# Moving the low-half subtraction of the first block's input-projection weights from VectorE to GpSimd

## What is computed

```python
def hybrid_mixer(x, w_in, sc_conv_w, attn_sink, cc_conv_w, cc_conv_b, cc_ln_g, cc_ln_b, w_out):
    z = x @ w_in                                   # 1024 x 2048
    sc_b, sc_c, sc_h, q, k, v, cc_a, cc_gate = jnp.split(z, IN_OFFSETS, axis=-1)
    y_sc = sc_b * depthwise_conv(sc_c * sc_h, sc_conv_w)          # 3 taps
    q, k = rope(q), rope(k)
    y_att = banded_window_attention(q, k, v, attn_sink)           # 8 heads, window 128
    u = cc_a * jax.nn.sigmoid(cc_gate)
    u = depthwise_conv(u, cc_conv_w) + cc_conv_b                  # 31 taps
    y_cc = jax.nn.silu(layer_norm(u, cc_ln_g, cc_ln_b))
    return jnp.concatenate([y_sc, y_att, y_cc], axis=-1) @ w_out
```

## Time and profile before

| | |
|---|---|
| median of three runs | 3438.07 us |
| the profiled execution, first to last instruction | 3433.0 us |
| rest of the device time, as median less span | 5.1 us |
| TensorE busy | 3345.7 us (97%) |
| VectorE busy | 1783.2 us (52%) |
| ScalarE busy | 1340.6 us (39%) |
| GpSimd busy | 62.8 us (2%) |
| first mixer, from its norm to the next MLP | about 370 to 560 us |
| second mixer | about 1317 to 1505 us |

### The profile page before, as it was taken

The page is one execution under the profiler, slowest core; times in us unless marked ns, Lnnn a source line. Parts: engine busy times, 40 slices in busy tenths (PEclk is TensorE's granted clock), DMA queues, the critical chain, the costliest instruction groups (busy, mean ns, idle before and its releaser), DMA issues.

```text
span 3433.0 us, 38143 instructions
## 1 busy us (share of the span) xinstructions
PE 3345.7 (97%) x15584; PEld 2742.5 (80%) x15584; DVE 1783.2 (52%) x2728; ACT 1340.6 (39%) x2144; POOL 62.8 (2%) x65
## 2 busy tenths in 40 slices
PE   9999989999999999899999999999999989999999
PEld 7888767888888887678888788777888778778887
DVE  4333785533363337855433775647444765655443
ACT  3222555322242225553322554434322565434332
POOL 0000100000000001000000000000000000000000
PEclk9999999999999999999999999999999999999999
DMA  5332311333333333123333333222333313223332
GB/s 159 98 98 88 85 50 56 105 98 98 93 90 100 94 91 87 47 59 105 108 95 92 92 92 105 86 59 80 104 95 96 86 56 98 69 62 105 98 98 68
DMA packets 604286, 304.10 MB, mean 89 GB/s; under 512 B 43600, under 2 KB 601808, under 8 KB 603984
## 3 DMA queue, kind: packets, MB, share of 16 engines
q1 hardware_dynamic: 604112, 301.66, 30.7%
HBM read 299.52 MB, written 2.10 MB: 88 GB/s over the span
## 4 chain that ended last, share of the span: by engine, by line
PE 82%; DVE 10%; ACT 6%; issue 1%; DMA 0%; SPq 0%; DVEq 0%; ACTq 0%
PE ps L1762 26%; PE ps L1763 25%; PE ps L1770 25%; DVE Y L2345 1%; DVE wl L2170 1%; DVE tmp L2179 1%; ACT wh L1944 1%; PE ps L1778 1%; PE ps L1929 1%; PE ps L1913 1%; ACT tmp L2021 1%; PE ps L1831 1%; ACT tmp L2014 1%; DVE HLa L2174 0%; ACT HHa L1950 0%
## 5 line engine op out<-in xcount | busy, mean ns | idle before, releaser
L1770 PE MATMUL ps<-XL,wh 128*128 128x512 f32 (+1 forms) x2856 | 1059.5, 381 | 0.5 <-DVE XL L2246 0.5
L1762 PE MATMUL ps<-XH,wh 128*128 128x512 f32 (+1 forms) x2624 | 1044.2, 399 | 15.3 <-DVE wl L2170 6.6
L1763 PE MATMUL ps<-XH,wl 128*128 128x512 f32 (+1 forms) x2624 | 1016.8, 388 | 0.0
L2170 DVE TENSOR_TENSOR wl<-raw,wh 128x1024 fp32r<-128x1024 f32 (+1 forms) x565 | 681.8, 1210 | 536.0 <-ACT wh L1944 535.4
L1944 ACT ACTIVATE wh<-raw 128x1024 fp32r<-128x1024 f32 (+1 forms) x565 | 585.3, 1039 | 566.6 <-PE ps L1770 537.0
L1770 PEld LDWEIGHTS ps<-XL,wh 128*128 128x128 f32 x2856 | 537.1, 188 | 104.7 <-DVE XL L2246 1.1
L1762 PEld LDWEIGHTS ps<-XH,wh 128*128 128x128 f32 x2624 | 494.2, 188 | 132.7 <-issue 14.7
L1763 PEld LDWEIGHTS ps<-XH,wl 128*128 128x128 f32 x2624 | 494.3, 188 | 99.5 <-issue 3.3
L1762 PE MATMUL ps<-HHa,wh 128*128 128x512 f32 x1088 | 428.2, 394 | 5.8 <-DVE HLa L2174 5.8
L1763 PE MATMUL ps<-HHa,wl 128*128 128x512 f32 x1088 | 423.7, 389 | 0.0
L1770 PE MATMUL ps<-HLa,wh 128*128 128x512 f32 x1088 | 407.9, 389 | 0.0
(11 more groups left out here) (333 smaller groups left out, 3066.5 us busy)
## 6 DMA issues: line engine op xcount, KB each, us to landing
raw<-in_ffn_w_gu SPq DMA_DIRECT2D x176, 512.0 KB, 3.8
raw<-in_w_ff SPq DMA_DIRECT2D x128, 512.0 KB, 4.1
raw<-in_ffn_w_down SPq DMA_DIRECT2D x64, 512.0 KB, 3.9
raw<-in_w_xkv SPq DMA_DIRECT2D x32, 512.0 KB, 3.9
raw<-in_ev_w_in SPq DMA_DIRECT2D x25, 512.0 KB, 3.9
raw<-in_ffn_w_down SPq DMA_DIRECT2D x32, 384.0 KB, 3.4
raw<-in_w_in SPq DMA_DIRECT2D x24, 512.0 KB, 3.9
raw<-in_w_out SPq DMA_DIRECT2D x64, 128.0 KB, 2.7
```

What stands on the lines that cost most here:

```text
L1762: e.matmul(bank[:, c], t.wh[u % SPL][:, k, :], h[:, c], start=first, stop=False, skip_group_check=True)
L1763: e.matmul(bank[:, c], t.wl[u % SPL][:, k, :], h[:, c], start=False, stop=False, skip_group_check=True)
L1770: m = e.matmul(bank[:, 0:n], t.wh[u % SPL][:, k, :], l, start=False, stop=last, skip_group_check=True)
L2170: self.e.tensor_tensor(wl, raw, f32(wh), ALU.subtract).then_inc(self.s["lo"], self.tag("lo", f"lo.{i}"))
```

## The change

For units of `w_in` the low-half subtraction is emitted by `Pool.split_unit` and no longer by `Vector.split_unit`. It signals on a semaphore of its own, `lop`. All other weights keep their subtraction on VectorE. `p_zero` on GpSimd waits in addition for all earlier subtractions of GpSimd. With 16 units in each of two layers, 32 of the 565 subtractions move.

```diff
+LOW_ON_POOL = ("w_in",)
-SEMS = ["mm", "pe", "hi", "act", "lo", "dve", "pool", ...]
+SEMS = ["mm", "pe", "hi", "act", "lo", "lop", "dve", "pool", ...]
@@ class Pool
+    def split_unit(self, i):
+        nk, r, s = self.units_in[i][3], i % RAW, i % SPL
+        if self.units_in[i][0] not in LOW_ON_POOL:
+            return
+        wh, wl, raw = (x[:, 0:nk, :] for x in (self.t.wh[s], self.t.wl[s], self.t.raw[r]))
+        self.hold.wait_ge(*self.at(f"hi.{i}"))
+        self.e.tensor_tensor(wl, raw, f32(wh), ALU.subtract).then_inc(self.s["lop"], self.tag("lop", f"lo.{i}"))
@@ Pool.p_zero
         self.hold.wait_ge(*self.own("pool"))
+        self.hold.wait_ge(*self.own("lop"))
         self.e.memset(ap, 0.0).then_inc(self.s["pool"], self.tag("pool", k))
@@ class Vector, split_unit
+        if self.units_in[i][0] in LOW_ON_POOL:
+            return
```

More of the change, by code:

```diff
@@ L193, in vec @@
         return self.VT[:, V_OFF[name] + i:V_OFF[name] + i + 1]
-SEMS = ["mm", "pe", "hi", "act", "lo", "dve", "pool", "ct", "mem", "out", "rga", "rgb", "pos"]
+SEMS = ["mm", "pe", "hi", "act", "lo", "lop", "dve", "pool", "ct", "mem", "out", "rga", "rgb", "pos"]
 SEMS += [f"raw{i}" for i in range(RAW)] + [f"x{k}" for k in range(KD)]
```

## The result

| | median | runs | ratio to before | 95% interval |
|---|---|---|---|---|
| before | 3437.33 us | 4 | | |
| changed | 3452.89 us | 4 | 1.0043 | 1.0031 to 1.0056 |

The changed kernel is 15.6 us slower; 3453 had been forecast. Its profiled execution has a span of 3449.9 us, 16.9 more than before. One execution, of 17298 us in the run with quarters for the 6th to 13th unit, is left out of its ratio.

The account below looks back on a forecast made before the run. TensorE was taken to bound the whole span, but in the mixers the chain through VectorE and ScalarE. Per mixer 1.5 + 0.2 + 3 + 2.9 = 7.6 us, 15 us for both, gave 3453 us, range 3430 to 3478.

Parts of the forecast that it names:

- The mutual exclusion: In the mixers, a GpSimd subtraction holds up VectorE's two-SBUF-input work for its 2.5 us, less one-input work or idle time.
- PSUM-reading instructions named as free: Masked maximum L2321, L2189, L2224 and L2306 read one operand from PSUM and should pass beside GpSimd's subtraction.
- one-input work: VectorE instructions with one input were to run unhindered under GpSimd's subtraction, shortening the 2.5 us hold-up.
- The price of a subtraction: One 128x1024 subtraction on GpSimd was put at 2.3 to 2.6 us, taken as 2.5, twice VectorE's 1.23.
- mean over 2.5 us: Sign of being right: GpSimd's group of subtractions has a mean over 2.5 us.
- The end of the MLP: GpSimd's last sum for the mean queues behind the third unit's subtraction, delaying VectorE's closing sum: +1.5 us a mixer.
- the worst rival: Full stalls: taps always pay the full time, or TensorE, idling more, loses clock; 3470 us, chance 0.13.
- Start of the projection: The fourth subtraction would end at about 393.6, TensorE wants it at 393.5: +0.2 us a mixer.
- 401 to 428 us: Subtractions from the sixth unit on stall rotations, the first score and centring, less VectorE's savings: +3 us a mixer.
- 428 to 519 us: Six units, eleventh to sixteenth, stalls less savings, the eleventh worst (+1.3), the thirteenth best (-0.25): +2.9 us a mixer.
- 9.0 us of relief: Eight of a mixer's sixteen subtractions stand on the chain at 1.13 us each; moving them frees at most 9.0 us.
- 14.9 us of stalls: VectorE standing still beside GpSimd's subtractions from 401 us on, per mixer: 14.9 us, 5.9 net of relief.

Follow-up runs that it names:

- the run with quarters for the 6th to 13th unit: Changed kernel, but only the 6th to 13th w_in unit of a layer subtracted on GpSimd, in four pieces of 256 columns; others on VectorE: 3435.8 us.
- the run without reads: Changed kernel, but for w_in units GpSimd writes zeros into the low-half tile (four half clears) instead of subtracting: 3427.6 us, ratio 0.9973.
- eighths: Changed kernel, but first three w_in units on VectorE and 4th to 16th on GpSimd in eight pieces of 128 columns: 3435.5 us, ratio 0.9991.

## Why the prediction was right

**The mutual exclusion** was the step on which the sign hung, and it held: 3427.6 us without the reads, 3452.9 with them. The PSUM-reading instructions named as free passed; the masked maximum (17 of them from 400 to 530 us in `tmp<-ps,CT`) kept 483 ns. That they should pass was the author's estimate, with no row beside it. The trace of the kernel before has such a case, GpSimd with four copies and VectorE with a subtraction that reads PSUM:

```profile
2897.89 2.30 POOL L2157 COPY M<-XM 128x512 f32<-128x512 f32 x4 [218.27 <-PE ps L1831]
```

```profile
2898.38 0.69 DVE L2174 TENSOR_TENSOR HLa<-ps,HHa 64x512 fp32r<-64x512 f32 x1 [9.79 <-ACT HHa L1950]
```

It took 0.69 us, the median of the 48 of this kind. What the prediction had wrong is that one-input work passes too: two such instructions took 2.09 us for 0.49 and 2.26 us for 0.23, as shown below. The prediction and the expectations speak of a port; the runs show that the two engines exclude each other (2.78 us for 0.69), and not by what.

**The price of a subtraction** was taken as 2.5 us. The fastest took 2.36, the median was 2.40, and the mean of 2.48 contains GpSimd's own waits for VectorE: eight of the 32 took 2.55 to 2.85 us. The mean over 2.5 us that was named as a sign of being right did not come, the other signs did.

**The end of the MLP** is the mis-sized term: 1.5 us forecast, 2.3 and 3.4 measured. The wait was right: the last sum ends late and the closing sum waits for it.

```profile
370.28 1.26 POOL L2156 TENSOR_TENSOR tmp<-tmp,XR 128x512 f32<-128x512 f32 x1
...
371.58 0.43 DVE L2193 TENSOR_TENSOR tmp<-tmp,XR 128x256 f32<-128x256 f32 x1 [1.51 <-POOL tmp L2156]
```

VectorE's row says 371.58 for 370.34, with the whole trace 0.2 us earlier at this point: 1.4 us. What I left out was the clock: behind this wait TensorE's granted clock fell to 0.50 (374 to 376 us). I had named the clock only in the worst rival.

**Start of the projection:** 0.2 us forecast, 0.0 measured in both. The fourth subtraction took 2.4 us and was in time.

**401 to 428 us:** +3 forecast, +2.6 in both. The walk was right in its order: L2328 2.78 us, then L2322 1.85, then L2328 again 2.76, then a centring sum 2.40.

**428 to 519 us:** +2.9 forecast, +3.8 and +1.8. The two mixers run the same instructions and differ by 2 us, so agreement here is partly luck. Their granted clock differs: worked out as length times what lacks to 1.00 over windows of 4 us (340 to 600 and 1290 to 1550 us), the clock cost 5.1 us of TensorE time before, 15.4 in the changed kernel, and 8.6 with eighths. Not all of it is on the chain, since TensorE is often waiting in these stretches. How much of the differences behind 463 us is the clock was not separated by a run.

**Two terms that were wrong in opposite directions.** The forecast took 9.0 us of relief for a mixer and set 14.9 us of stalls against them (5.9 net from 401 us on). The run without reads puts the relief at 6.2 us only. The mixers lost 4.8 and 6.0 us between the norm and the next MLP, so the stalls cost 11.1 and 12.2 us there, as an estimate from these two runs. Both terms were some 3 us too large. Why is open; part of VectorE's time may not be on the chain, whether it is saved or lost. That the two errors cancelled is at least in part luck.

**What was wrong in the working and did not show in the sum.** The prediction let one-input work pass. VectorE's bias instruction at the sixteenth unit (L2347 before, L2361 after) did not:

```profile
490.34 2.40 POOL L2151 TENSOR_TENSOR wl<-raw,wh 128x1024 fp32r<-128x1024 f32 x1 [4.20 <-ACT wh L1947]
...
490.93 2.09 DVE L2361 TENSOR_SCALAR M<-M,VT 128x512 f32<-128x512 f32 x1
```

It stood still until about 492.5, for a 0.49 us instruction. Had it passed, the tap behind it would have stood still for most of that time instead; that would explain why the sum hardly moved, but no run separates the two.

**The sum:** 15 us forecast, 16.9 in the profiled execution, 15.6 by the medians. Too little at the MLP's end (by 2.7 for both) and a little too much in the middle (0.8 from 401 to 428 us, and 0.3 at the start). The rest of the 16.9 us, behind 428 us and outside the mixers, is about what was forecast for it.

## What to carry to other kernels

An engine at 2% is not free if its instructions hold up the one to be relieved. Before moving an elementwise step to GpSimd, list what VectorE runs in that stretch. What began inside a whole subtraction of GpSimd here stood still until about its end if it had two SBUF inputs (L2328, 2.78 us for 0.69), or one input and its output in SBUF (L2361, 2.09 us for 0.49); what read an operand from PSUM kept its length (L2320, 0.69 us). Here each moved subtraction saved 1.1 us of VectorE's time and stalled it for 0.4 to 2.1 us. If the step must go there, cut it into pieces: of 256 columns they gave 3436.9 us and of 128 columns 3435.5, where whole subtractions gave 3448.4 and pieces of 64 columns 3439.1. And look at what stands behind it in GpSimd's own queue. A wait of 1.6 us on TensorE cost another 0.9 and 2.0 us in clock here (granted clock 0.50); a few filler products in the gap kept it at 1.00.

## What the runs showed of the hardware beyond that

VectorE instructions with one tensor input can be blocked as well. The bias instruction above is one (2.09 us for 0.49); the other is tiny:

```profile
443.75 2.38 POOL L2151 TENSOR_TENSOR wl<-raw,wh 128x1024 fp32r<-128x1024 f32 x1 [7.24 <-ACT wh L1947]
...
443.90 2.26 DVE L2340 TENSOR_SCALAR sm<-sm,CT 128x4 f32<-128x4 f32 x1
```

Four columns, 0.23 us before, took 2.26 us. Both instructions read one tensor in SBUF and write into SBUF, and in the second mixer they took 2.08 and 2.26 us. A few columns are enough.

It also shows that the clears are not quite free. In the run without reads the bias instruction began 0.13 us after a clear:

```profile
481.66 0.52 POOL L2154 MEMSET wl<- 128x512 f32 x1
481.79 0.67 DVE L2366 TENSOR_SCALAR M<-M,VT 128x512 f32<-128x512 f32 x1
```

It took 0.67 us for 0.49, and the one on four columns 0.38 for 0.23, while the 36 instructions with two SBUF inputs that began inside one of these clears kept their time to 0.01 us. So the prediction's sentence that a clear shows no effect holds for two SBUF inputs only.

A short instruction is not let through first in these traces: the one on four columns took 2.26 us for 0.23. A piece of 64 columns on GpSimd took 0.31 us at the least and 1.97 at the most, so GpSimd waits for VectorE too: in 16 pieces it spent 430 ns on the mean for one.
